# Prompt attention with unnormalised probabilities as two-part weights of 128-column value products

## What is computed

```python
s = jnp.einsum('bqhd,bkhd->bhqk', qblk, k).astype(jnp.float32) * ATTN_SCALE
s = jnp.where(kpos[None, :] <= qpos[:, None], s, -jnp.inf)
p = jax.nn.softmax(s, axis=-1).astype(v.dtype)
return jnp.einsum('bhqk,bkhd->bqhd', p, v)
```

## Time and profile before

| what | value |
|---|---|
| median of three runs | 2110.39 us |
| the profiled execution | 2108.73 us |
| its span, first to last instruction | 2107.0 us |
| mean granted TensorE clock in it | 0.960 of 2.4 GHz |
| PE busy / weight loads busy | 2002.8 us (95%) / 1877.5 us (89%) |
| VectorE / ScalarE / GpSimd busy | 928.2 / 796.6 / 428.4 us |

### The profile page before, as it was taken

The page is one execution under the profiler, slowest core; times in us unless marked ns, Lnnn a source line. Parts: engine busy times, 40 slices in busy tenths (PEclk is TensorE's granted clock), DMA queues, the critical chain, the costliest instruction groups (busy, mean ns, idle before and its releaser), DMA issues. The chain is left out here.

```text
span 2107.0 us, 38039 instructions
## 1 busy us (share of the span) xinstructions
PE 2002.8 (95%) x13358; PEld 1877.5 (89%) x13358; DVE 928.2 (44%) x1679; ACT 796.6 (38%) x1702; POOL 428.4 (20%) x391
## 2 busy tenths in 40 slices
PE   6999997999969999999999698899999999999998
PEld 5999985777749999999998496799999999999998
DVE  6125145556536777777777622521222222221222
ACT  5012134656635666666666311311121111212121
POOL 3233133111010000010000323331222222231221
PEclk7999998999979999999999598899999999999999
DMA  6122000000022222222222111020202011120202
GB/s 213 50 64 63 10 19 9 1 1 0 0 71 63 77 74 73 70 75 73 74 69 107 40 40 29 22 61 26 75 15 65 25 55 50 30 61 24 75 15 97
DMA packets 180599, 108.42 MB, mean 51 GB/s; under 512 B 52132, under 2 KB 177154, under 8 KB 180276
## 3 DMA queue, kind: packets, MB, share of 16 engines
q1 hardware_dynamic: 180358, 107.21, 17.7%
q10 hardware_dynamic: 174, 0.30, 0.1%
HBM read 97.47 MB, written 10.00 MB: 51 GB/s over the span
## 5 line engine op out<-in xcount | busy, mean ns | idle before, releaser
L1750 PE MATMUL banks<-comb_hi,pageT_hi 128*128 128x272 f32 x1024 | 234.3, 310 | 0.0
L1640 DVE TENSOR_REDUCE k_sums<-k_sq 128x8 f32<-128x512 f32 x256 | 174.4, 681 | 92.3 <-ACT k_sq L1462 92.3
L1750 PE MATMUL banks<-comb_hi,pageT_lo 128*128 128x272 f32 x1024 | 212.5, 289 | 0.0
L1750 PE MATMUL banks<-comb_lo,pageT_hi 128*128 128x272 f32 x1024 | 212.2, 289 | 0.0
L1462 ACT ACTIVATE k_sq<-banks 128x512 f32<-128x512 f32 x256 | 152.0, 594 | 142.4 <-PE banks L1750 139.4
L2045 DVE TENSOR_TENSOR xT<-xT,banks 128x1074 f32<-128x1074 f32 x64 | 81.5, 1274 | 277.4 <-PE banks L244 277.4
L2035 DVE TENSOR_TENSOR relu_squared<-relu 128x1074 f32<-128x1074 f32 x32 | 40.9, 1278 | 305.2 <-ACT relu L1949 305.2
L1949 ACT ACTIVATE relu<-banks 128x1074 f32<-128x1074 f32 x32 | 34.3, 1071 | 360.3 <-PE banks L244 351.9
L244 PE MATMUL banks<-a_hi,w_down_hi 128*128 128x358 f32 x768 | 168.2, 327 | 0.0
L244 PE MATMUL banks<-a_hi,w_down_lo 128*128 128x358 f32 x768 | 167.7, 326 | 0.0
L244 PE MATMUL banks<-a_lo,w_down_hi 128*128 128x358 f32 x768 | 167.6, 326 | 0.0
(11 more groups left out here) (371 smaller groups left out, 4044.3 us busy)
## 6 DMA issues: line engine op xcount, KB each, us to landing
page_latents<-in_cache_kv_latent SPq DMA_DIRECT2D x256, 128.0 KB, 2.1
w_up_raw<-in_w_up SPq DMA_DIRECT2D x32, 512.0 KB, 4.2
w_down_raw<-in_w_down SPq DMA_DIRECT2D x64, 256.0 KB, 2.8
w_in_raw<-in_w_in SPq DMA_DIRECT2D x17, 512.0 KB, 3.8
x_spill<-xT SPq DMA_DIRECT2D x1, 4296.0 KB, 13.9
xT<-x_spill SPq DMA_DIRECT2D x1, 4296.0 KB, 12.8
page_ropes<-in_cache_k_rope SPq DMA_DIRECT2D x256, 16.0 KB, 1.8
w_o_raw<-in_w_o SPq DMA_DIRECT2D x8, 512.0 KB, 4.2
```

The source lines that it names most:

```text
L1640: nc.vector.tensor_reduce(ksum[par][:, j, :], sq[j % 2][:, :].rearrange("p (h c) -> p h c", h=H), AX_X, ALU.add)\
L1750: mm = pe.matmul(banks[:, 2 * (j % 2) + half, 0:WC], x[j % AHEAD][:, k, :], w[par][:, k, half, :], start=k == 0 and a == 0, stop=k == KL - ...
```

## The change

The probabilities are no longer normalised before they are turned. ScalarE copies a turned chunk as fp32r (`probsT_hi`), VectorE subtracts that from the turned chunk (`probsT_lo`), and both become weights of 128 x 128; the moving operand is a block of values split in the same way, 64 high columns and 64 low ones side by side (`v_head_split`, made by GpSimd with two more instructions a head and a second product). The output of a tile is then 128 queries x 128 columns in bank 7; ScalarE scales the low half by the reciprocal of the row sum (`out_low`), VectorE scales the high half and adds (`out_tokens`). Units and chunks share banks 5 and 6 by turns, as numbered jobs. At the end of the last head `out_tokens` is turned back into `attnT`, with 36 transposes and nine copies. Every tile keeps 128 rows, the ninth too (`rows = lambda t: P`). The last value product of a head now runs in the next head's tile 0.

```diff
-    pt = [ar.take(f"probsT{i}", [P, 4, P], F32) for i in range(2)]
+    pt_hi, pt_lo = ([ar.take(f"{n}{i}", [P, 4, P], F32R) for i in range(2)] for n in ("probsT_hi", "probsT_lo"))
...
-    vh = [ar.take(f"v_head{i}", [P, NT, VH], F32) for i in range(2)]
+    vf = ar.take("v_head", [P, NT, VH], F32)
+    vh = [ar.take(f"v_head_split{i}", [P, NT, 2 * VH], F32R) for i in range(2)]
+    part = [ar.take(f"out_low{i}", [P, VH], F32) for i in range(2)]
+    out_tok = ar.take("out_tokens", [P, NT, AW], F32)
...
+                nc.gpsimd.tensor_mul(vh[par][:, :, 0:VH], g.v_tok[:, :, ds(n * VH, VH)],
+                                     g.inv_kv[:, 0:NT].unsqueeze(2).broadcast_to([P, NT, VH])).then_inc(s["v_high"], 1)
...
+                nc.gpsimd.tensor_sub(vh[par][:, :, VH:2 * VH], vf[:, :, :], vh[par][:, :, 0:VH].bitcast(F32))\
+                    .then_inc(s["v_head_ready"], 1)
...
-                        act.copy(pt[(par + c) % 2][:, 0:m, :], banks[:, 6, 0:m * P].rearrange("p (j q) -> p j q", q=P))\
-                            .then_inc(s["p_copied"], 1)
+                        act.copy(split_keys(pt_hi[(par + c) % 2], t, m), turned_keys(job_bank(n, par, in_head(t, c, last)), t, m))\
+                            .then_inc(s["hi_done"], 1)
                         c += 1
                         if j == 0 and t >= 1:
-                            keep_output(n, par, t - 1)
+                            scale_low(n, t - 1, par + t - 1)
...
+            def keep_output(n, t, scaled):
+                v.wait_ge(s["out_scaled"], LEAD + n * NT + (t + 1))
+                nc.vector.scalar_tensor_tensor(out_tok[0:rows(t), t, ds(n * VH, VH)], banks[0:rows(t), OUT_BANK, 0:VH], ri[0:rows(t), t:t + 1],
+                                               part[scaled % 2][0:rows(t), :], ALU.mult, ALU.add).then_inc(s["out_done"], 1)
...
                     v.wait_ge(s["exped"], LEAD + n * NT + (t + 1))
-                    pr = probs[(par + t) % 2][:, 0:(t + 1) * P]
-                    nc.vector.tensor_scalar(pr, pr, ri[:, t:t + 1], None, ALU.mult).then_inc(s["normed"], 1)
...
+                    for j, m in chunks(t):
+                        v.wait_ge(s["hi_done"], LEAD + job_of_chunk(n, t, c, last) + 1)
+                        nc.vector.tensor_sub(split_keys(pt_lo[(par + c) % 2], t, m),
+                                             turned_keys(job_bank(n, par, in_head(t, c, last)), t, m),
+                                             split_keys(pt_hi[(par + c) % 2], t, m).bitcast(F32)).then_inc(s["split"], 1)
+                        c += 1
+                        if j == 0 and t >= 1:
+                            keep_output(n, t - 1, par + t - 1)
...
+            def values(n, par, t, c, j, m, last):
+                pe.wait_ge(s["split"], LEAD + job_of_chunk(n, t, c, last) + 1)
                 if j == 0:
-                    pe.wait_ge(s["out_copied"], LEAD + n * NT + t)
+                    pe.wait_ge(s["out_done"], LEAD + n * NT + t)
...
                 for x in range(m):
-                    mm = pe.matmul(banks[0:VH, 7, 0:P], vh[par][:, j + x, :], pt[(par + c) % 2][:, x, :],
-                                   start=j + x == 0, stop=j + x == t)
+                    k = slice(0, rows(j + x))
+                    pe.matmul(banks[0:rows(t), OUT_BANK, 0:2 * VH], hi[k, x, :], vh[par][k, j + x, :], start=j + x == 0, stop=False)
+                    mm = pe.matmul(banks[0:rows(t), OUT_BANK, 0:2 * VH], lo[k, x, :], vh[par][k, j + x, :], start=False, stop=j + x == t)
...
-                        pe.wait_ge(s["p_copied"], LEAD + n * NCH + c)
+                        pe.wait_ge(s["split"], LEAD + job - 1)
```

More of the change, by code:

```diff
@@ L1011, in before, with job_of_unit, job_of_chunk, job_bank @@
         return sum(len(chunks(x)) for x in range(t)) - sum(len(chunks(NT + x)) for x in range(t, 0))
+    UNIT_AT = lambda t: t - 1 if 1 <= t <= NU else None
+    NJ = NCH + NU
+    def job_of_unit(n, u):
+        return NU + n * NJ + (before(u + 1) + u)
+    def job_of_chunk(n, t, c, last):
+        return NU + n * NJ + (c if last else c + min(t, NU))
+    def job_bank(n, par, at):
+        return 5 + (at + par * NJ) % 2
+    in_head = lambda t, c, last: c if last else c + min(t, NU)
     def score_shape(t):
@@ L1164, in head @@
-                    if not last and 1 <= t <= NU:
-                        split_lo(n + 1, 1 - par, t - 1)
+                        maxima(n + 1, t + 2 - NT)
+                    if not last and UNIT_AT(t) is not None:
+                        u = UNIT_AT(t)
+                        unit_low(n + 1, 1 - par, u, job_bank(n, par, before(t) + u), job_of_unit(n, u))
+                    for j, m in chunks(t):
[6 more added lines that the diff above has]
+                            keep_output(n, t - 1, par + t - 1)
+                        elif j == 0 and not first:
+                            keep_output(n - 1, LAST, 1 - par + LAST)
@@ L1167, in _ @@
+                if last:
+                    keep_output(n, LAST, par + LAST)
+                    for t in range(1, NT, 2):
+                        v.wait_ge(s["out_turned"], t + 1)
+                        nc.vector.tensor_copy(g.attnT[:, :, t * P:t * P + kept(t)],
+                                              banks[:, t % 4, :].rearrange("p (k q) -> p k q", q=P)[:, :, 0:kept(t)])\
+                            .then_inc(s["out_copied_dve"], 1)
             heads(v, head)
@@ L1211, in head @@
                     for u in range(NU):
-                        transpose_unit(0, u, u)
-                    score(0, 0, 0)
-                    score(0, 0, 1)
-                pe.wait_ge(s["v_head_ready"], n + 1)
-                c, behind = 0, None
+                        turn_unit(0, u, u, u)
+                    score(0, 0, 0, NU)
+                    score(0, 0, 1, None)
+                c, behind = 0, None if first else (n - 1, 1 - par, LAST, NCH - 1, *chunks(LAST)[-1], False)
                 for t in range(NT):
@@ L1218, in head @@
                     if t + 2 < NT:
-                        score(n, par, t + 2)
+                        score(n, par, t + 2, None)
                     elif not last:
-                        score(n + 1, 1 - par, t + 2 - NT)
-                    if not last and 1 <= t <= NU:
-                        transpose_unit(n + 1, t - 1)
-                    pe.wait_ge(s["normed"], n * NT + (t + 1))
+                        score(n + 1, 1 - par, t + 2 - NT, job_of_unit(n, NU - 1) + 1 if t + 2 == NT else None)
@@ L1231, in head @@
+                        mm.then_inc(s["turned"], 1)
                         if behind:
-                            values(n, par, *behind)
-                        behind = (t, c, j, m)
+                            values(*behind)
+                        behind = (n, par, t, c, j, m, last)
                         c += 1
-                values(n, par, *behind)
+                if last:
+                    values(*behind)
+                    for t in range(NT):
+                        pe.wait_ge(s["out_done"], LEAD + n * NT + (t + 1))
+                        if t >= 4:
+                            if t % 2 == 0:
+                                pe.wait_ge(s["out_copied_act"], (t - 4) // 2 + 1)
+                            else:
+                                pe.wait_ge(s["out_copied_dve"], (t - 4) // 2 + 1)
+                        for k in range(AW // P):
+                            mm = pe.transpose(banks[:, t % 4, k * P:k * P + rows(t)], out_tok[0:rows(t), t, k * P:(k + 1) * P],
+                                              ident[0:rows(t), 0:rows(t)])
+                        mm.then_inc(s["out_turned"], 1)
```

172 lines of the change are left out of this document (104 added, 68 removed).

## The result

The changed kernel took 2177.88 us (median of four runs, 2147.80 to 2193.99) against 2110.66 for the kernel before on the same chip: slower, ratio 1.0218 with a 95% interval of 1.0148 to 1.0287. The medians stand 1.032 apart; the ratio is taken over the two faster executions of the changed kernel alone (2147.80 and 2164.50). The forecast had the direction, but 2121 us and a range to 2138 were far too low. The mean granted clock over the whole execution falls as the time grows: 0.948, 0.937, 0.923 and 0.923 for the four, from the fastest to the slowest, against 0.960 in the profiled execution of the kernel before. The profiled execution of the changed kernel took 2191.25 us, its span is 2189.5; it is one of the two with the lowest clock, so what follows shows the loss at its larger size.

The account below looks back on a forecast made before the run. TensorE was taken as the bound, with VectorE's serial chain holding it in tiles 4 to 8 after the change. Seven heads +5.8 us and last head and end +4.5 on 2108.7, median 1.7 above: 2121 us, range 2109 to 2138.

Parts of the forecast that it names:

- No loss where weights keep their shape: TensorE, tiles 0 to 3: losses of 0.13 us a value product and 0.09 ahead of it go with 128-column weights.
- The rival that the losses stay: Shape isn't what costs the 0.13 and 0.09 us; they remain with the new weights: about 2137 us, chance 0.09.
- A product at 0.11 us: Each fp32r value product on TensorE costs 0.11 us (bound 0.125), so four blocks cost 0.88 us as before.
- a product would have taken 0.17: Rival: weights aren't loaded under running products, load 0.11 plus stream 0.06 us each; 2155 us, chance 0.03.
- Scores lose their 0.11: TensorE's scores: the uncovered first weight load becomes covered, saving 0.11 us for each tile's scores.
- The chain through VectorE in tiles 4 to 8: Scores, maxima, low parts, output, product become serial: 5.31, 5.66, 5.32, 3.55 and 4.67 us for tiles 4 to 8.
- The rival that TensorE stays the bound: VectorE's waits are covered, saving 4.3 us a head: about 2081 us, faster; chance 0.14.
- The end: Behind the last head's last block: 36 transposes of 0.11 us and a last copy, 4.36 us.
- the same sum: Seven heads 0.83 us longer each, +5.8 us, plus 4.5 for last head and end: +10.3 us.
- the last sign of being wrong: Among the signs that would show the forecast wrong: a granted clock under 1.00 in the phase.
- the rival "the clock falls": The granted clock drops from 1.00 in the phase, some 18 us for each head hit; 2139 us for one, chance 0.05.
- "one head": How many heads the half clock was priced for: one, some 18 us, giving 2139 us.

Follow-up runs that it names:

- half-widened run: The changed kernel with only the product with the high part reading its 128 value columns twice; 2137.7 us, ratio 1.0123 to the kernel before.
- filled run: The changed kernel with idle fp32r products of 256 columns put into TensorE's waits of tiles 4 to 8; 2129.1 us, ratio 1.0092 to the kernel before.
- widened kernel: The changed kernel with both value products of a block reading their 128 value columns twice; 2132.7 us, ratio 1.0110 to the kernel before.
- the order: The changed kernel with scores of tile t+2 and their maxima moved behind the first chunk's transposes in tiles 4 to 8; 2121.4 us, ratio 1.0048.
- with idle products: The changed kernel with scores and maxima moved in tiles 4 to 8, idle products in TensorE's longest waits, early output transposes in the last head; 2109.4 us, ratio 1.0000.

## Why the prediction was right about the direction and wrong about the size

Its steps, at the full clock. The tile lengths are distances between the first score rows of the kernel after (384.15, 392.13, 397.49, 404.10, 411.06, 414.77, 419.57), with the one product that fell to the low clock at the end of tile 5 put back (1.74 less 0.92); tile 6 stood at the low clock there and is taken from the half-widened run (469.00 to 474.42, below), whose six products with the high part in it are wider, some 0.08 us too long by estimate (six times 0.129 less 0.115).

| part of a head, us | forecast | measured |
|---|---|---|
| tiles 0 to 3 | 7.79 | 7.98 |
| tile 4 | 5.31 | 5.36 |
| tile 5 | 5.66 | 5.79 |
| tile 6 | 5.32 | 5.42 |
| tile 7 | 3.55 | 3.71 |
| tile 8 | 4.67 | 4.80 |
| head | 32.30 | 33.06 |

```profile
469.00 0.39 PE L1275 MATMUL banks<-k_hi,q_hi 96*128 96x384 f32 x1
...
474.42 0.27 PE L1275 MATMUL banks<-k_hi,q_hi 96*128 96x128 f32 x1
```

- *No loss where weights keep their shape*: right. Transposes to product 0.35 where 0.53 stood, a product of eight 0.92 where 1.01 stood. The rival that the losses stay is out. That it was the shape, and not the float32 type of the old products, no run separates.
- *A product at 0.11 us*: 0.115, inside its bounds. Behind a wait a product of eight still takes 0.92 us, where the forecast had 0.88 and 0.11 for a load that can't be covered. Weights are loaded under running products: loads are counted at 0.19 us each, and the products follow each other every 0.115. By the Trainium skill's rule that a load overlaps only when it goes to other rows of the array ("TensorE: Matmul & The Clock Gate", Part 3, what overlaps and what doesn't) a product would have taken 0.17, as the forecast estimated; the trace does not agree.
- *Scores lose their 0.11*: only half right. Scores of 448 columns take 1.40 (392.13 to 393.53) against 1.46; that is most of what tiles 0 to 3 missed.
- *The chain through VectorE in tiles 4 to 8*: right in place and order, and in price within 0.05 to 0.16 us a tile; the waits for its output are the first row of PE's waits. The rival that TensorE stays the bound is out at this order.
- *The end*: 4.36 forecast behind the last block, 4.4 measured (672.59 to 676.96).

With 33.06 for 32.30 the same sum gives seven times 1.59, and 4.5 at the end: about 16 us, 2126, inside the range; the filled run's 2129 stands near it, at 1.0092 of the kernel before, so the direction was no luck. From there to the median of 2178 (2148 to 2194 by execution) it is the clock, which the sum took at 1.00 throughout; a granted clock under 1.00 in the phase was the last sign of being wrong that the prediction named. **The step that failed is the rival "the clock falls", given 0.05**, in two places. Its condition was read from busy time: PE at "about 26 of 32 us" was weighed against 26 of 44 and seemed safe. But busy share does not separate the cases here: 20.79 of 23.90 us was followed by a fall, while 28.57 of 33.60 held in the widened kernel. Beside the waits there are the new products, which by the prediction's own estimate stream for 0.06 us of the 0.115 that each takes; that was priced in time only. And its reach: "one head" at 18 us. Heads two and three lost 3 to 4 us each (36.3 and 36.8 for 33.1), all later ones 10 to 11. That is less than 18 because the clock was down for two thirds of a head and not for all of it, and because part of the longer work ran into waits that were there anyway (PE is idle 2.8 us of a head of 44.3, and 5.0 in the widened kernel at 1.00). The clock as a likely case, five heads at 11 on top of 2126, would have given about 2181.

What stays open is what exactly the chip weighs: these runs show that waits and short products add up, and that the edge is near (two heads of the same instructions, one at 1.00, one at 0.81), not where it lies. Nor does a run separate what lets the old product keep the clock better: it too moves 128 columns a record, but in float32 and behind 64 columns of weights. That a longer stream brings the clock back is shown; that a shorter one is the difference between old and new is not.

## What to carry to other kernels

When an edit gives TensorE short products and more waits at once, forecast the granted clock as a term of its own, and read it by windows in the first profile, since PE's busy time rises when the clock falls (41.5 of 44.3 us here). Filling waits with idle products, or reading a moving operand twice, is a cheap test: it tells clock from chain in one run, and here brought the ratio to the kernel before from 1.022 to 1.009 and 1.011. The larger part of the cure was the order, which alone came to 1.005 and with idle products to 1.000: independent TensorE work belongs between a chunk's transposes and the product that waits for them, but only in the tiles that have that wait.

## What the hardware showed that was not expected

- The half-clock stretches are the busiest ones: 26.85 of 27.30 us busy at 0.50, and the clock did not return for 27 us. Being busy at the low clock did not raise it soon. The Trainium skill ("TensorE: Matmul & The Clock Gate", Part 1) lets the gate follow how busy the array has been; PE's busy share in the profile does not show that here.
- A value product with 256 moving columns costs 0.129 us (eight of them 1.03 in the widened kernel, 500.45 to 501.48), one with 128 columns 0.115: at the full clock twice the stream costs 12%, so widening costs little time, and it kept the clock in most heads. The first of the eight and the scores behind the last:

```profile
500.45 0.36 PE L1288 MATMUL banks<-v_head_split,probsT_hi 128*128 128x256 f32 x1 [0.44 <-DVE out_tokens L1207]
...
501.48 0.34 PE L1275 MATMUL banks<-k_hi,q_hi 96*128 96x384 f32 x1
```
